# Opening a third and a fourth output-projection unit in further PSUM banks, modulation blocks behind the results, and the MLP square from PSUM

## The reference, cut to what matters

```python
h = h + (o * jax.nn.silu(gate)) @ w_out_a[i]      # layer A, then the same with w_out_b in layer B
...
c_act = jax.nn.silu(c)
mod = c_act @ ada_w[l] + ada_b[l]                 # 1024 x 6144
sh1, sc1, g1, sh2, sc2, g2 = ... jnp.split(mod, N_MOD, axis=-1)
h = rmsnorm_2(x, norm_mix_w[l]) * (1.0 + sc1) + sh1
mix = jnp.concatenate([o_a, o_b, o_c], axis=-1) @ w_out[l]
x = x + g1 * mix
h = rmsnorm_2(x, norm_mlp_w[l]) * (1.0 + sc2) + sh2
ff = jnp.square(jax.nn.relu(h @ mlp_w1[l])) @ mlp_w2[l]
x = x + g2 * ff
```

## Time and profile before

| what | value |
|---|---|
| median of 3 runs | 1379.73 us (1379.16 to 1382.02) |
| the profiled execution's own time | 1389.31 us |
| its span | 1387.5 us |
| PE busy | 1274.5 us (92% of the span) |
| DVE / ACT / POOL busy | 718.9 / 671.2 / 380.4 us |
| mean granted TensorE clock | 0.964 of full speed |
| DMA | 127.47 MB, mean 92 GB/s |

### The profile page before, as it was taken

One profiled execution on the slowest core, in us unless ns is written; L12 is line 12 of the kernel. 1 busy time (PEld: TensorE's weight loads), 2 busy tenths in 40 slices (PEclk: granted clock), 3 DMA queues, 4 the chain that ended last, 5 costly groups with the idle time before them and its releaser, 6 DMA issues.

```text
span 1387.5 us, 18246 instructions
## 1 busy us (share of the span) xinstructions
PE 1274.5 (92%) x6720; PEld 986.2 (71%) x6720; DVE 718.9 (52%) x1396; ACT 671.2 (48%) x1247; POOL 380.4 (27%) x192
## 2 busy tenths in 40 slices
PE   7899999998989999879998799887878999999995
PEld 4677777776757776657765687675657888888884
DVE  3566655557765666554897645555755122121223
ACT  5566666664437676434656675552243133132231
POOL 2000000004300000323676674121324435344350
PEclk9999999999999999989999999988989999999998
DMA  4312222236331221443121011113624223233221
GB/s 154 127 61 77 77 76 77 76 100 205 121 90 62 78 92 46 153 136 99 61 75 47 17 47 49 44 31 120 213 85 158 92 88 109 77 105 106 83 99 61
DMA packets 37235, 127.47 MB, mean 92 GB/s; under 512 B 4624, under 2 KB 5520, under 8 KB 37152
## 3 DMA queue, kind: packets, MB, share of 16 engines
q1 hardware_dynamic: 33984, 120.34, 26.4%
q10 hardware_dynamic: 3168, 6.03, 1.4%
HBM read 122.91 MB, written 2.13 MB: 90 GB/s over the span
## 4 chain that ended last, share of the span: by engine, by line
PE 69%; DVE 12%; issue 10%; ACT 6%; DMA 1%; POOL 1%; DVEq 0%; SPq 0%; ACTq 0%; POOLq 0%
PE G L596 17%; PE G L597 17%; PE G L598 17%; PE S L705 2%; PE S L1347 2%; PE O L766 2%; PE T L745 1%; PE S L928 1%; PE N L631 1%; PE O L991 1%; DVE S L576 1%; DVE adaw L2323 1%; PE T L975 1%; DVE best L2322 1%; DVE sq L505 1%
## 5 line engine op out<-in xcount | busy, mean ns | idle before, releaser
L596 PE MATMUL G<-hi,wH 128*128 128x512 f32 x1360 | 569.1, 418 | 47.0 <-DVE lo L566 15.4
L422 POOL TENSOR_TENSOR wL<-w,wH 128x1024 fp32r<-128x1024 f32 x122 | 298.4, 2449 | 931.0 <-ACT wH L1570 930.9
L597 PE MATMUL G<-lo,wH 128*128 128x512 f32 x1360 | 538.5, 396 | 0.0
L598 PE MATMUL G<-hi,wL 128*128 128x512 f32 x1360 | 538.0, 396 | 0.0
L596 PEld LDWEIGHTS G<-hi,wH 128*128 128x128 f32 x1360 | 260.5, 192 | 131.8 <-issue 48.3
L597 PEld LDWEIGHTS G<-lo,wH 128*128 128x128 f32 x1360 | 261.3, 192 | 57.2 <-issue 8.4
L598 PEld LDWEIGHTS G<-hi,wL 128*128 128x128 f32 x1360 | 260.5, 192 | 57.7
L1570 ACT ACTIVATE wH<-w 128x1024 fp32r<-128x1024 f32 x170 | 179.0, 1053 | 164.6 <-PE G L598 136.7
L695 DVE CUSTOM_DVE_ANT_0 adaw<-adaw,scr 128x1024 f32<-128x1024 f32 x48 | 81.4, 1702 | 52.3 <-issue 52.3
L678 DVE SCALAR_TENSOR_TENSOR xT<-G,modT,xT 128x512 f32<-128x512 f32 x40 | 30.0, 750 | 135.6 <-PE G L598 135.6
L2025 ACT ACTIVATE tmp<-G 128x512 f32<-128x512 f32 x32 | 19.1, 598 | 128.6 <-PE G L598 128.6
(11 more groups left out here) (348 smaller groups left out, 1553.1 us busy)
## 6 DMA issues: line engine op xcount, KB each, us to landing
w<-weights_dram SPq DMA_DIRECT2D x170, 512.0 KB, 3.5
adaw<-ada_dram SPq DMA_DIRECT2D x48, 512.0 KB, 4.4
kd<-c_dram ACTq DMA_DIRECT2D x8, 512.0 KB, 3.5
xT<-x_dram SPq DMA_DIRECT2D x4, 512.0 KB, 7.6
out_dram<-xT SPq DMA_DIRECT2D x8, 256.0 KB, 2.2
scr<-ca_dram SPq DMA_DIRECT2D x2, 512.0 KB, 4.3
kd<-cbias ACTq DMA_DIRECT2D x8, 128.0 KB, 2.4
adaw<-steps_dram SPq DMA_DIRECT2D x1, 384.0 KB, 4.0
```

The costliest lines, as they stand in the source:

```text
L422: g.tensor_tensor(wL[:, u.slot], w32[:, u.slot % 2], wH[:, u.slot].bitcast(f32), ALU.subtract).then_inc(w_lo, 1)
L596: mm(G[u.bank][:, :], whi, H[:, k, :], start=(k == first), stop=False)
L597: mm(G[u.bank][:, :], whi, L[:, k, :], start=False, stop=False)
L598: last = mm(G[u.bank][:, :], wlo, H[:, k, :], start=False, stop=(k == final))
```

## The change

1. **A further bank.** In all three projections unit 2 accumulates in `T[0]`, in layer C unit 3 in `T[1]` too (`output_home`); `T[0]` and `T[1]` are then free of the last head's transposes. PE opens unit 2 behind unit 1 on all tiles but the last (in layer C unit 2, and tiles 4 to 7 of unit 3), and closes 0, 1 and 2 when the last tile is there. Unit 3 then waits for the result of unit 1 in A and B; in layer C units 4 and 5 wait for those of 0 and 1, units 6 and 7 for those of 4 and 5.
2. **Modulation blocks behind the results.** `add_output` runs a unit's blocks after its add and square, and the table moves them from (2, 2, 1, 1, 1, 1, 1, 1) to (0, 0, 2, 2, 2, 2, 2, 0), in layer C from (2, 2, 2, 2, 1, 1, 1, 1) to (0, 0, 2, 3, 3, 2, 2, 0). SP's queue follows the same table.
3. **The MLP's square from PSUM.** DVE multiplies `tmp` (relu) by `G` itself instead of by `tmp`, so that a bank is free at the square (`f_sq`) and no longer at the relu; in quarter 0 the block comes behind the square and the low part.

The diff:

```diff
@@ -89,8 +89,8 @@
 
 ADA_OA, ADA_B, ADA_OB, ADA_OM, ADA_M = 0, 10, 18, 28, 40
 
-ADA_PER = {"a": (ADA_OA, (2, 2, 1, 1, 1, 1, 1, 1)), "b": (ADA_OB, (2, 2, 1, 1, 1, 1, 1, 1)),
-           "m": (ADA_OM, (2, 2, 2, 2, 1, 1, 1, 1))}
+ADA_PER = {"a": (ADA_OA, (0, 0, 2, 2, 2, 2, 2, 0)), "b": (ADA_OB, (0, 0, 2, 2, 2, 2, 2, 0)),
+           "m": (ADA_OM, (0, 0, 2, 3, 3, 2, 2, 0))}
 
 
 def wait(eng, sem, value):
@@ -584,7 +584,8 @@
             norm_root(dve, link, key)
             norm_rows(dve, key)
 
-        def gemm(pe, u, H, L, free, h_ready=None, part=range(KT), first=0, final=KT - 1):
+        def gemm(pe, u, H, L, free, h_ready=None, part=range(KT), first=0, final=KT - 1, home=None):
+            home = G[u.bank] if home is None else home
             if part[0] == first:
                 pe.wait_ge(w_lo, u.n + 1)
                 if free is not None:
@@ -593,9 +594,9 @@
                 if h_ready is not None:
                     pe.wait_ge(h_ready[0], h_ready[1] + k + 1)
                 whi, wlo = wH[:, u.slot, k, :], wL[:, u.slot, k, :]
-                mm(G[u.bank][:, :], whi, H[:, k, :], start=(k == first), stop=False)
-                mm(G[u.bank][:, :], whi, L[:, k, :], start=False, stop=False)
-                last = mm(G[u.bank][:, :], wlo, H[:, k, :], start=False, stop=(k == final))
+                mm(home[:, :], whi, H[:, k, :], start=(k == first), stop=False)
+                mm(home[:, :], whi, L[:, k, :], start=False, stop=False)
+                last = mm(home[:, :], wlo, H[:, k, :], start=False, stop=(k == final))
             if part[-1] == final:
                 last.then_inc(gemm_done, 1)
 
@@ -663,24 +664,31 @@
             v.tensor_tensor(L[:, bass.ds(t, 1), :], og[:, :].unsqueeze(1), H[:, bass.ds(t, 1), :].bitcast(f32),
                             ALU.subtract).then_inc(sem(f"{ph}_gated_lo"), 1)
 
+        def output_home(ph, n, u):
+
+            if ph != "f" and n == 2:
+                return T[0]
+            return T[1] if ph == "m" and n == 3 else G[u.bank]
+
         def add_output(dve, ph, unit, gate=None, key=None):
 
             for n in range(KT):
-                if ph in ADA_PER:
-                    base, per = ADA_PER[ph]
-                    for b in range(sum(per[:n]), sum(per[:n + 1])):
-                        ada_block(dve, Block(base, b), {"a": 16, "m": 32}.get(ph) if b == 0 else None)
                 u = unit(n)
                 dve.wait_ge(gemm_done, u.n + 1)
+                home = output_home(ph, n, u)
                 if gate is None:
-                    v.tensor_tensor(xT[:, n, :], G[u.bank][:, :], xT[:, n, :], ALU.add).then_inc(sem(f"x_{ph}"), 1)
+                    v.tensor_tensor(xT[:, n, :], home[:, :], xT[:, n, :], ALU.add).then_inc(sem(f"x_{ph}"), 1)
                 else:
-                    v.scalar_tensor_tensor(out=xT[:, n, :], in0=G[u.bank][:, :], scalar=modT[:, gate + n:gate + n + 1],
+                    v.scalar_tensor_tensor(out=xT[:, n, :], in0=home[:, :], scalar=modT[:, gate + n:gate + n + 1],
                                            in1=xT[:, n, :], op0=ALU.mult, op1=ALU.add).then_inc(sem(f"x_{ph}"), 1)
                 if key and n:
                     add_square(dve, key, n - 1)
                 if key == "kv" and n:
                     scaled_low(dve, key, n - 1)
+                if ph in ADA_PER:
+                    base, per = ADA_PER[ph]
+                    for b in range(sum(per[:n]), sum(per[:n + 1])):
+                        ada_block(dve, Block(base, b), {"a": 16, "m": 32}.get(ph) if b == 0 else None)
             if key:
                 add_square(dve, key, KT - 1)
             if key == "kv":
@@ -1126,8 +1134,9 @@
                 gemm(pe, unit_az(n), hi1, lo1, mark("a_raw1", n + 2) if n < 7 else mark("a_vraw", 8), part=part)
 
             def output_a(n, part):
-                gemm(pe, Unit(UOA, n), hi2, lo2, mark("x_a", n - 1) if n > 1 else mark("a_zraw", 7 + n),
-                     mark("a_gated_lo", 0) if n < 2 else None, part=part)
+                u = Unit(UOA, n)
+                gemm(pe, u, hi2, lo2, [mark("a_zraw", 7), mark("a_zraw", 8), mark("a_pT_out", 47)][n] if n < 3 else mark("x_a", n - 1),
+                     mark("a_gated_lo", 0) if n < 3 else None, part=part, home=output_home("a", n, u))
 
             gemm_a(0, 0, range(KT))
             gemm_a(0, 1, range(KT))
@@ -1177,9 +1186,10 @@
                 if more:
                     turn_v(n + 1)
             output_a(1, range(7))
-            output_a(0, (7,))
-            output_a(1, (7,))
-            for n in range(2, 8):
+            output_a(2, range(7))
+            for n in range(3):
+                output_a(n, (7,))
+            for n in range(3, 8):
                 output_a(n, range(KT))
 
 
@@ -1217,8 +1227,9 @@
                 gemm(pe, unit_z(n), hi2, lo2, free, part=part)
 
             def output_b(n, part):
-                gemm(pe, Unit(UOB, n), hi1, lo1, mark("x_b", n - 1) if n > 1 else mark("b_zraw", 7 + n),
-                     mark("b_gated_lo", 0) if n < 2 else None, part=part)
+                u = Unit(UOB, n)
+                gemm(pe, u, hi1, lo1, [mark("b_zraw", 7), mark("b_zraw", 8), mark("b_pT_out", 31)][n] if n < 3 else mark("x_b", n - 1),
+                     mark("b_gated_lo", 0) if n < 3 else None, part=part, home=output_home("b", n, u))
 
             turn_bk(0)
             turn_bv(0)
@@ -1264,9 +1275,10 @@
             mix_b(pe, 7, 1)
             spread_b(pe, 7)
             output_b(1, range(7))
-            output_b(0, (7,))
-            output_b(1, (7,))
-            for n in range(2, 8):
+            output_b(2, range(7))
+            for n in range(3):
+                output_b(n, (7,))
+            for n in range(3, 8):
                 output_b(n, range(KT))
             norm_tensor(pe, "mix")
 
@@ -1434,7 +1446,9 @@
                 for name, count, tiles in (("c_gated_lo", 2, (4, 5)), ("cv_gated_lo", 2, (6, 7)), ("h_gated_lo", part[-1] + 1, (0, 1, 2, 3))):
                     if part[-1] in tiles:
                         pe.wait_ge(sem(name), count + since(name))
-                gemm(pe, Unit(UOM + n), hi1, lo1, mark(["h_raw2", "h_raw3"][n], 4), part=part, first=4, final=3)
+                u = Unit(UOM, n)
+                gemm(pe, u, hi1, lo1, [mark("h_raw2", 4), mark("h_raw3", 4), mark("h_state", 12), mark("h_aT", 23)][n], part=part,
+                     first=4, final=3, home=output_home("m", n, u))
 
             def fill(t, k):
 
@@ -1540,20 +1554,23 @@
             outputs(3)
             output_m(1, (2,))
             sum_h(3)
-            output_m(0, (3,))
-            output_m(1, (3,))
-            for n in range(2, 8):
-                gemm(pe, Unit(UOM, n), hi1, lo1, mark("x_m", n - 1))
+            output_m(2, (4, 5, 6, 7, 0, 1, 2))
+            output_m(3, (4, 5, 6, 7))
+            for n in range(3):
+                output_m(n, (3,))
+            output_m(3, (0, 1, 2, 3))
+            for n in range(4, 8):
+                gemm(pe, Unit(UOM, n), hi1, lo1, mark("x_m", n - 1 if n > 5 else n - 3))
 
             norm_tensor(pe, "mlp")
 
             def quarter(c):
                 first = isinstance(c, int) and c == 0
                 for n in range(8):
-                    free = (mark("x_m", 7 + n) if first else mark("x_f", c * 8 + (n - 1))) if n < 2 else mark("f_relu", c * 8 + (n - 1))
+                    free = (mark("x_m", 7 + n) if first else mark("x_f", c * 8 + (n - 1))) if n < 2 else mark("f_sq", c * 8 + (n - 1))
                     gemm(pe, Unit(UM, n, c, 16), hi2, lo2, free, mark("lo_mlp", 0) if first and n == 0 else None)
                 for n in range(8):
-                    free = mark("x_f", c * 8 + (n - 1)) if n > 1 else mark("f_relu", c * 8 + (7 + n))
+                    free = mark("x_f", c * 8 + (n - 1)) if n > 1 else mark("f_sq", c * 8 + (7 + n))
                     gemm(pe, Unit(UM, 8 + n, c, 16), hi1, lo1, free, mark("f_lo", c * 8) if n == 0 else None)
             repeated(pe, 3, quarter)
             quarter(3)
@@ -2494,17 +2511,17 @@
             def quarter(c, key=None):
                 for n in range(9):
                     if n < 8:
-                        if isinstance(c, int) and c == 0:
-                            ada_block(dve, Block(ADA_M, n))
-
+                        u = Unit(UM, n, c, 16)
                         dve.wait_ge(sem("f_relu"), c * 8 + (n + 1))
                         wait(dve, sem("f_lo"), c * 8 + (n - 1))
-                        v.tensor_tensor(T[n % 2][:, :], tmp[:, n % 2, :], tmp[:, n % 2, :], ALU.mult
+                        v.tensor_tensor(T[n % 2][:, :], tmp[:, n % 2, :], G[u.bank][:, :], ALU.mult
                                         ).then_inc(sem("f_sq"), 1)
                     if n:
                         wait(dve, sem("f_hi"), c * 8 + n)
                         v.tensor_tensor(lo1[:, n - 1, :], T[(n - 1) % 2][:, :], hi1[:, n - 1, :].bitcast(f32),
```

(2 more changed lines are left out.)

## The result

The change made the kernel slower. The median went from 1379.73 us (1379.16 to 1382.46 in five runs) to **1391.59 us** (1387.46 to 1395.78, five runs), a ratio of 1.0064 [1.004, 1.0088]. Repeated later beside other runs of the kernel before, it was 1392.98 against 1382.47 us, 1.0073 [1.0049, 1.0097]. The forecast was 1377.6 us with a range up to 1384.0.

What follows compares the result with a forecast made beforehand. It took PE's matmul stream as the bound, with DVE's line of blocks ending each projection. A -1.3, B +1.7, C +3.1 and MLP quarter 0 -5.6 sum to -2.1 us: median 1379.73 to 1377.6 us, range 1371.0 to 1384.0.

Steps and rivals of the forecast that it cites:

- What bounds the kernel: PE's stream of matmuls, busy 92% of the span; time is to be had only in its waits, 19.3 us.
- the late line of blocks: Projections: DVE's modulation blocks, loaded only behind unit 6's weights, end last in all three; A -1.3, B +1.7, C +3.1 us.
- the waits inside the projections: Sign of being right: new PE waits inside the projections, several us before unit 6 in C, released by xT.
- The pace P = 6.4: Projections: 6.4 us from one pair of blocks to the next; each tenth moves the sum by 1.3 us.
- The rival that had the change slower: Projections: late landings set the pace; from P = 6.8 the sum exceeds +2.8, at 7.0 1385.4 us; chance 0.17.
- lower end of 4.5: Least P, one landing and one block (3.3 + 1.2); near it the change would be some 12 us faster.
- The last pair takes 2.4: End of each projection: 2.4 us for the last two blocks; in A 6.3 us in all to the norm matmul.
- With the median of 4.4 the first lands: Projections: first block lands 4.4 us after issue, at 326.7 in A, 587.2 in B, 970.5 in C.
- The base: Difference of -2.1 us worked out on the profiled execution, 1389.31 us, then applied to the median, 1379.73 us.
- MLP quarter 0, -5.6: MLP quarter 0: the place costs 7.0 us; 1.4 of PE's wait stays and the clock stays up, gaining 5.6.

Runs made afterwards that it cites:

- the control: The kernel before, unchanged, run and profiled once more: 1.0007 of the kernel before in the runs beside it, median 1383.79 us.
- the best order of them: Changed kernel with the first two blocks loaded ahead of unit 5's weights and summed behind the second result: 0.9981 of the kernel before, 1379.63 us.
- the one with a short line and two banks: The spread kernel with part 1 taken back in all three layers: 0.986 of the kernel before, 1362.34 us.
- the further matmuls around the norms: The spread kernel with 8 further matmuls ahead of the norm matmuls of B and C and 24 behind them: 0.9883 of the kernel before, 1367.42 us.
- the spread kernel: Changed kernel with first blocks loaded and summed earlier, 8 blocks per projection, eight moved to B's heads: 0.9889 of the kernel before, 1368.34 us.
- the spread kernel with the banks in C alone: The spread kernel with part 1's further banks kept only in layer C: 0.9845 of the kernel before, 1362.01 us.

## Why the prediction was wrong

**What bounds the kernel; that the late line of blocks matters: right.** With the line shortened by less data or shorter sums, 20 to 23 us came off the changed kernel; an earlier start and fewer blocks together took off 25. B and C became longer as forecast (A too, against the forecast), and the waits inside the projections that it named are there.

**The pace P = 6.4: right in size, not the error.** The rival that had the change slower asked for a P from 6.8 on; the change was slower, and not by that. In the profile after, the first blocks of pairs were 6.54 us apart in A (326.76 to 352.90, four steps), 5.86 in B (590.52 to 613.96) and 6.15 in C (969.56 to 1000.33, five steps). Two readings beside it are off, without weight for the sum: C does have a pair that comes 4.8 us behind the one before it (960.87 to 965.69; the earlier trace rows shows the second), though that step starts from blocks loaded ahead; and a P near its lower end of 4.5 would by the prediction's own terms bring some 23 us (13 steps of 1.9, less 2 where PE would end A), not 12.

**"The last pair takes 2.4": mis-sized, the largest error.** The step took both landings as done and only two sums of 1.2 us as left. The two loads of a pair are no pair in time: the second leaves only when the second sum before it is done. From the last pair's first block to the eighth result it was 4.2 us in B (613.96 to 618.14), and 4.2 in C. In B the first block of that pair took 2.90 us beside POOL's split, but that is not what put the second off, whose load landed at 616.9. In A it was 3.75 us, as the second block started at 355.51; the rest of its stretch to the norm matmul, 8.5 instead of 6.3, is three matmuls of 1.45 us in place of 0.7 at the lower level of the clock (0.79 us listed), behind the wait of 3.39. That is 1.8 + 1.8 + 1.4 = 5.0 us for the second buffer and 0.8 for the clock. The second blocks of the last pairs:

```profile
355.51 1.22 DVE L703 CUSTOM_DVE_ANT_0 adaw<-adaw,scr 128x1024 f32<-128x1024 f32 x1 [1.38 <-issue]
...
1003.39 1.22 DVE L703 CUSTOM_DVE_ANT_0 adaw<-adaw,scr 128x1024 f32<-128x1024 f32 x1 [1.46 <-issue]
```

The pace of *pairs* was right, and the tail behind it was too short by the lag of the second buffer. The other two profiles with the same code in the projections have tails of 4.0 and 4.4 us in B, 4.2 and 4.6 in C; in A one has 4.0 and the other 2.3, so there the lag is not always there.

**"With the median of 4.4 the first lands": too short in B.** The first load took 6.2 us there; C's came 0.9 late. That is 2.8 us, offset in part by P below 6.4 in B and C (2.2 and 1.2). Altogether A missed by 2.9, B and C by 1.5 each.

**The base: an execution longer than most.** The forecast added its difference to the median, but took its rows from an execution of 1389.31 us. In the control B took 44.3 and C 42.4 us, where the first profile had 45.6 and 43.7. Against the control the loss of the projections is 11.4 us where the first pair of profiles shows 9.4.

**MLP quarter 0, -5.6: right alone (5.6 in the profile, 5.1 in the medians), 4.5 to 4.8 within the change.** The wait left was 1.05 us, 1.4 forecast, and the clock stayed up. That the fall of the clock would be there to save was chance: of five profiles without the part the matmul behind the wait is listed with 0.79 or 0.80 us in three, and with 0.50 in two.

**What was weighed too lightly.** The late start was costed for each part together, and nowhere was it asked what part 1 is worth in A and B by itself. By the forecast's own working it costs 4.8 us in each and saves nothing, as the wait it fills is one that the blocks in front of the result made, and part 2 takes those away. Without it the change was even (1.0003).

In all: -2.1 forecast; +5.9 for the projections' misses, +1.0 for the MLP, +2.0 for the base are +6.8 us. Measured are +8.8 and +10.1 (0.0064 and 0.0073 of 1382). The rest, 2 to 3 us, no profile shows, and its cause stays open: both profiled executions of the changed kernel were the fastest of their series.

## To carry to other kernels

A wait of the busiest engine that a change fills is a gain only if nothing behind the work that fills it is thereby late; ask of each stage separately whether the engine stood still there for want of data or of a buffer. A chain through two buffers ends one lag later than its pace says: count from the last buffer's own load, not from the pair's first. And when work of fixed length hangs in a stage that it makes last, also try to move some of it to a stage that has room: here eight blocks moved to layer B's heads were worth as much again as the best order of them (0.0092 each).

## What the runs showed of the hardware

**Within one kernel the time goes with the granted clock.** In 35 runs of the kernel before, the fastest was 1377.86 us with a mean granted clock of 0.969, the slowest 1391.03 with 0.961. Span times clock is 1333.3 and 1335.0, and between 1329.8 and 1337.5 in all 35: a spread of 0.6% where the times spread by 1%. For the one with a short line and two banks it is 1320.9 to 1323.4. It does not always part two kernels: for the changed kernel it is 1335.6 to 1341.7 in its first series and 1339.7 to 1345.6 in the second, and the first overlaps with before. Nor does it measure what sets the time: with the further matmuls around the norms it rose (1333.4 to 1335.1, where the spread kernel has 1327.5 to 1330.4), and the time stayed.

**The same waits leave different clocks.** Layer C's heads took 338 us in some profiles and 344.6 in others, with nearly the same waits of PE: the difference is in its busy time, 303.0 of 338.1 us in the changed kernel and 309.4 of 344.6 in the spread kernel with the banks in C alone (1926 and 1928 matmuls), at a mean granted clock of 0.95 and 0.93. Below is the stretch behind a wait of 1.69 us (for L837) in the control of before, and of 1.70 us in the kernel with the MLP part alone, which is the same code up to there:

```profile
704.31:714.31 10.00, 8.49 (x26) 5.74 (x27) 9.55 (x31) 7.58 (x18) 7.33 (x6) 0.66 0.08 23
```

```profile
702.74:712.74 10.00, 7.97 (x36) 5.37 (x35) 9.55 (x33) 7.58 (x18) 6.36 (x5) 1.00 0.01 2
```

0.66 is a clock of 1.2 GHz in two thirds of the stretch and 2.4 in the rest. The page "TensorE: Matmul & The Clock Gate" of the Trainium skill, part 1, says that the observation on which the gate acts runs free of the kernel's start, so that the place of a change differs between runs. These two rows agree in that one execution has the fall and the other has not; why, they don't show. Profiles of two kernels are therefore to be compared by stages and waits, and only then by their length.
